# RWKV recurrence on one core: the first group's levels start after its first scores; its transposes and second scores run between them

## The chip, the core and the metric

One of the eight cores of a Trainium2 chip runs the whole kernel. The metric is the device time of one execution in microseconds, the median of several. The engines are TensorE (PE; its weight loads are listed as PEld), VectorE (DVE), ScalarE (ACT), GpSimd (POOL) and SyncE (SP), which issues the DMAs. Each engine works through its own queue in order and waits for the others by semaphores.

## What is computed

A stack of layers over 272 tokens (16 meta tokens and 256) of width 1024: feed-forward blocks, one RWKV-7 time mix, a sparse attention, and a mixer of retention, convolution and block-sparse attention. The change touches only the recurrence of the time mix, for 16 heads of 64:

```python
def step(S, inp):
    r_t, w_t, k_t, v_t, a_t, b_t = inp
    sa = jnp.einsum("bhij,bhj->bhi", S, a_t)
    S = S * w_t[:, :, None, :] + sa[..., None] * b_t[:, :, None, :] + v_t[..., None] * k_t[:, :, None, :]
    y = jnp.einsum("bhij,bhj->bhi", S, r_t)
    return S, y
```

Here `a_t` is minus the normalised key and `b_t` the same key times a gate. To the output `y` a normalisation, a bonus term `sum(r * k * r_k) * v` and a gate are applied, and then the matrix `rk_o`.

## The kernel before, in words

**Tiling.** The recurrence is computed in chunks of tokens, `CHUNKS`: chunk 0 has 16, chunks 1 and 2 have 128 each. Inside a chunk it is a linear system whose matrix is triangular; its inverse is built by doubling, in levels (`rk_levels`, 4 for chunk 0 and 7 for the others). The 16 heads are taken in four groups `g` of four heads (two tiles of 128 rows).

**What a group needs.** `rk_prepare(g)` on DVE scales the operands (five operations of 128x544). `rk_turn(g, c)` on PE transposes six tiles of a chunk into PSUM, and `rk_turned` on ACT copies them out in two copies. `rk_score(g, c, i)` on PE makes the products of the chunk: `i = 0` those from which the inverse is built, `i = 1` those used later, in the chain over chunks. `rk_mask(g, c, i)` on DVE masks each into SBUF. `rk_begin(g, c)` on DVE makes the first approximation of the inverse from the masked `i = 0` product.

**Levels.** In level `n`, `rk_under` (PE) is followed by a copy (ACT, level 0) or a mask (DVE, later), then `rk_merge` (PE) and additions (DVE). The order of chunks is `RK_ORDER = (1, 2, 0)`. `fill` issues dummy matmuls: four before each first product of group 0, and more before level 6. In the first group there are 33 steps on each engine: step 0 to 2 are level 0 (on DVE empty), 3 to 8 level 1 (three products, then three merges), 9 to 14 level 2, 15 to 20 level 3, and four each (chunks 1 and 2) for levels 4, 5 and 6. The first product of level 1 is `rk_under(0,1,1)` (group 0, chunk 1, level 1).

**Order beside the levels.** `beside(host, guest)` puts a second string of work between the steps of the first: the guest yields numbers (ticks), and what comes behind a yield of `k` is issued after step `k`. During the levels of group `g` the guests are the transposes, scores and masks of group `g + 1` and the chain of group `g - 1`. The order is fixed when the program is written; each engine issues it as a single queue.

**Banks.** PSUM has 8 banks. The levels use banks 0 to 4, `rk_banks` gives those of transposes and scores: 6 and 7, and for group 0 chunks 1 and 2 banks 0, 1 and 2, 3. The tiles of `rk_v` before use banks 0 to 2 and the bonus banks 4 to 7 (two halves of DVE's product, `rk_bonus_read`).

**Semaphores.** `rk_masked` counts masks in the order of `MASKS`; `masked(g, c, i)` is the count after that mask. `rk_mask` waits for `rk_products_ready`, before the change by the number `2 * (3 * g + c) + i + 1`.

**Around it.** Before the recurrence stand `rk_r` and `rk_v`, whose weights are split in two parts (`w_high` by ACT, `w_low` by POOL); behind its last group `rk_g2` and `rk_o`, and a feed-forward. The DMA ring of weights is refilled as PE uses slots.

## Time and profile before

| | |
|---|---|
| median of 3 runs | 2140.13 us (2139.15 to 2152.64) |
| profiled execution | 2132.1 us, its span 2130.3 us |
| mean granted TensorE clock | 0.978 of full |
| PE busy | 2013.0 us (94%) |
| DVE / ACT / POOL busy | 1055.2 / 922.0 / 1279.0 us |
| DMA moved | 291.96 MB, 137 GB/s on average |

The profile is that of one execution on the chip. It lists busy times by engine, windows of time with the busy share and the granted clock of TensorE (1.00 is 2.4 GHz, 0.50 is 1.2 GHz), and timelines of instructions. Start times count from the start of the span. Idle time before an instruction is in brackets with what released it. A helper's line (L1916, L1348) stands for many operations; they are told apart by tile and shape. One f32 matmul of the program is two instructions in the trace, so a score of four heads is x8 and an under of a 128-token chunk x16.

### The profile page before, as it was taken

What the parts mean: (1) busy time and instruction counts of PE and PEld (TensorE: products, weight loads), DVE (VectorE), ACT (ScalarE), POOL (GpSimd) and SP (SyncE); (2) the same over time, 40 slices, a digit from 0 to 9 for tenths busy, and PEclk for the clock granted to TensorE, in tenths of its full rate; (3) what the DMA queues carried; (4) which work ended last, traced back from release to release, by engine and by line L of the source; (5) the groups of instructions that cost most, each with busy time, mean ns of one, the idle gap of its engine ahead of it and who ended that gap; (6) DMA issues with size and microseconds to landing.
All of it is one profiled execution on the core that took longest, in us unless ns stands there. A gap on an engine that the chain in (4) does not pass through costs nothing.

```text
span 2130.3 us, 43769 instructions
## 1 busy us (share of the span) xinstructions
PE 2013.0 (94%) x17458; PEld 1896.2 (89%) x17458; DVE 1055.2 (50%) x1623; ACT 922.0 (43%) x1590; POOL 1279.0 (60%) x528
## 2 busy tenths in 40 slices
PE   7999798999999999999978999999999988999997
PEld 7999587778799999999865999989998877898997
DVE  5770766665668716860465577021263244324431
ACT  4333453111343344343436543444446555656552
POOL 6887253000278877786630688967656554677885
PEclk9999899999999999999989999999999999999999
DMA  6444132000244454454320355544354332343552
GB/s 267 170 175 175 73 138 80 3 3 2 80 158 177 166 174 157 177 180 174 125 74 1 139 177 185 192 176 158 125 210 142 139 112 90 135 179 140 191 185 77
DMA packets 40919, 291.96 MB, mean 137 GB/s; under 512 B 4432, under 2 KB 5712, under 8 KB 5712
## 3 DMA queue, kind: packets, MB, share of 16 engines
q1 hardware_dynamic: 40640, 288.92, 38.0%
q8 instruction: 108, 1.77, 0.3%
q10 hardware_dynamic: 144, 1.05, 0.1%
q14 instruction: 27, 0.22, 0.0%
HBM read 288.90 MB, written 1.05 MB: 136 GB/s over the span
## 4 chain that ended last, share of the span: by engine, by line
PE 31%; issue 28%; POOLq 19%; POOL 18%; ACT 1%; DVE 1%; DMA 0%; DVEq 0%; SPq 0%; ACTq 0%
POOLq L1894 18%; POOL w_low L1890 18%; PE ps L587 9%; PE ps L595 9%; PE ps L591 9%; PE ps L1283 1%; PE ps L1271 1%; PE ps L1261 1%; PE ps L699 0%; POOLq L1889 0%; DMA X<-x_in 0%; ACT units L1796 0%; ACT units L1348 0%; POOLq L1906 0%; DVE units L1916 0%
## 5 line engine op out<-in xcount | busy, mean ns | idle before, releaser
L1890 POOL TENSOR_TENSOR w_low<-wring,w_high 128x1024 fp32r<-128x1024 f32 x524 | 1278.8, 2455 | 830.1 <-ACT w_high L1348 800.8
L587 PE MATMUL ps<-in_high,w_high 128*128 128x256 f32 (+1 forms) x2856 | 829.1, 290 | 33.7 <-DVE in_low L1916 12.9
L595 PE MATMUL ps<-in_high,w_low 128*128 128x256 f32 (+1 forms) x2856 | 819.4, 287 | 0.0
L591 PE MATMUL ps<-in_low,w_high 128*128 128x256 f32 (+1 forms) x2856 | 819.3, 287 | 0.0
L1348 ACT ACTIVATE w_high<-wring 128x1024 fp32r<-128x1024 f32 x524 | 542.3, 1055 | 286.4 <-PE ps L587 281.8
L587 PEld LDWEIGHTS ps<-in_high,w_high 128*128 128x128 f32 x2856 | 545.1, 191 | 42.9 <-issue 37.3
L595 PEld LDWEIGHTS ps<-in_high,w_low 128*128 128x128 f32 x2856 | 545.7, 191 | 0.0
L591 PEld LDWEIGHTS ps<-in_low,w_high 128*128 128x128 f32 x2856 | 544.6, 191 | 0.5
L587 PE MATMUL ps<-hid_high,w_high 128*128 128x272 f32 (+1 forms) x880 | 254.9, 290 | 0.0
L595 PE MATMUL ps<-hid_high,w_low 128*128 128x272 f32 (+1 forms) x880 | 250.7, 285 | 0.0
L591 PE MATMUL ps<-hid_low,w_high 128*128 128x272 f32 (+1 forms) x880 | 250.5, 285 | 0.0
L1916 DVE TENSOR_TENSOR hid_low<-hidden,hid_high 128x272 f32 (+1 forms) x88 | 215.7, 2451 | 13.0 <-issue 2.6
L1919 DVE SCALAR_TENSOR_TENSOR X<-ps,X 128x272 f32<-128x272 f32 (+1 forms) x64 | 27.7, 433 | 333.8 <-PE ps L595 333.8
L591 PEld LDWEIGHTS ps<-hid_low,w_high 128*128 128x128 f32 x880 | 165.9, 189 | 0.7
L587 PEld LDWEIGHTS ps<-hid_high,w_high 128*128 128x128 f32 x880 | 165.7, 188 | 0.7
L595 PEld LDWEIGHTS ps<-hid_high,w_low 128*128 128x128 f32 x880 | 165.8, 188 | 0.0
L1490 ACT ACTIVATE silu_out<-ps 128x272 f32<-128x272 f32 (+1 forms) x88 | 34.7, 394 | 301.8 <-DVE ps L1916 301.8
L1954 DVE CAST hid_high<-hidden 128x272 f32 (+1 forms) x88 | 96.7, 1099 | 17.2 <-issue 17.2
L1916 DVE TENSOR_TENSOR ps<-ps,rms 128x272 f32<-128x272 f32 (+1 forms) x176 | 74.0, 436 | 61.6 <-PE ps L595 60.5
L1348 ACT ACTIVATE AL<-ps 128x272 f32<-128x272 f32 (+5 forms) x95 | 39.6, 433 | 142.2 <-PE ps L595 51.9
L1919 DVE SCALAR_TENSOR_TENSOR conv_out<-ps,par,conv_out 128x255 f32<-128x255 f32 x88 | 42.4, 482 | 47.0 <-ACT conv_out L1479 38.3
L1437 ACT ACTIVATE units<-ps 128x256 f32<-128x256 f32 x69 | 26.4, 383 | 85.1 <-PE ps L595 85.0
(331 smaller groups left out, 2580.6 us busy)
## 6 DMA issues: line engine op xcount, KB each, us to landing
wring<-stream SPq DMA_DIRECT2D x271, 1024.0 KB, 4.8
con<-consts SPq DMA_DIRECT2D x1, 2199.0 KB, 16.0
X<-x_in SPq DMA_DIRECT2D x1, 1088.0 KB, 7.6
units<-decay ACTq DMA_DIRECT2D x1, 1024.0 KB, 4.8
out<-AL SPq DMA_DIRECT2D x1, 1024.0 KB, 4.7
par<-params SPq DMA_DIRECT2D x1, 187.0 KB, 4.9
con<-consts SPq DMA_DIRECT2D x1, 130.0 KB, 7.5
```

The costliest lines, as they stand in the source:

```text
L587: mm = pe.matmul(o, wh, high(k), start=(k == 0), stop=False)
L591: mm = pe.matmul(o, wh, low(k), start=False, stop=False)
L595: mm = pe.matmul(o, wl, high(k), start=False, stop=(k == kt - 1))
L1261: mm = pe.matmul(heads(3)[:, q, 0:keys.shape[1]], ns_q[p:p + HD, 2 * g + u, c * P:(c + 1) * P], keys[p:p + HD, :], start=True, stop=True)
L1348: return act.activation(o, i, ACT.Copy, scale=scale)
L1437: act.activation(put(i), ps[:, BANK[tile], 0:size], func(i)).then_inc(S["act_emptied"], 1)
L1490: act.activation(silu_out[:, p % 2, tokens], ps[:, (base + 2 * p) % 4, 0:size], ACT.Silu).then_inc(S["act_emptied"], 1)
L1890: pool.tensor_tensor(w_low[:, (half + h) % SPLIT_RING, :], wring[:, slot, h * HALF * P:(h + 1) * HALF * P], w_high[:, (half + h) % SPLIT_R ...
L1894: pool.drain()
L1916: return dve.tensor_tensor(o, a, b, op)
L1919: return dve.scalar_tensor_tensor(out=o, in0=a, scalar=scalar, in1=b, op0=op0, op1=op1)
L1954: dve.tensor_copy(hid_high[:, tile, tokens], hidden[:, p:p + 1, tokens])
```

## The change

In group 0 the scores `i = 0` come first, in the order of chunks 1, 2, 0, for the first two without waiting for the bonus; DVE begins each chunk behind its mask, and takes the second half of the bonus product between chunk 2 and chunk 0. The transposes of group 0, its scores `i = 1` and their masks move between the levels of group 0, ahead of the same work for group 1, whose ticks move back. Transposes and second scores of all groups now use banks 6 and 7. ACT copies group 0's transposes behind its copies of level 0. DVE's `rk_prepare(1)` stands between the two halves of the bonus.

```diff
--- before.py
+++ after.py
@@ -420,13 +420,13 @@
             bank, at = ((4, 64 * i), (max(i - 1, 0), 0), (2 + max(i - 1, 0), 0))[c]
             return ps[0:C, bank, at:at + 4 * B].rearrange("p (q t) -> p q t", q=4)
 
-        def rk_banks(g, c):
-
-
-            return 6 if g else (6, 0, 2)[c]
-
-
-        MASKS = [(0, c, i) for i in range(2) for c in range(3)]
+        def rk_banks(g, c, i):
+
+
+            return 6 if g or i else (6, 0, 2)[c]
+
+
+        MASKS = [(0, c, 0) for c in RK_ORDER] + [(0, c, 1) for c in range(3)]
         MASKS += [(g, c, i) for g in range(1, 4) for c in range(3) for i in range(2)]
 
         def masked(g, c, i):
@@ -722,16 +722,14 @@
 
                 t0, C = CHUNKS[c]
                 now = slice(t0, t0 + C)
-                before = 3 * g + c
-                if g:
-                    pe.wait_ge(S["rk_masked"], 2 * before)
-                if c == 0:
+                pe.wait_ge(S["rk_masked"], masked(g, c, 0 if g else 1) - 1)
+                if c == 0 and g:
                     pe.wait_ge(S["rk_prepared"], g + 1)
                 settle(C)
                 for i, first in enumerate((32, 8, 16)):
                     for u in range(2):
                         n = 2 * i + u
-                        mm = pe.transpose(ps[0:C, rk_banks(g, c) + n // 4, n % 4 * P:(n % 4 + 1) * P],
+                        mm = pe.transpose(ps[0:C, 6 + n // 4, n % 4 * P:(n % 4 + 1) * P],
                                           A[:, first + 2 * g + u, now], ident)
                 mm.then_inc(S["rk_turned"], 1)
 
@@ -739,15 +737,16 @@
 
                 t0, C = CHUNKS[c]
                 now = slice(t0, t0 + C)
-                before = 3 * g + c
-                if i == 0:
-                    pe.wait_ge(S["rk_tm_copied"], before + 1)
+                if g == i == 0:
+                    pe.wait_ge(S["rk_prepared"], 1)
+                elif g == 0 or i == 0:
+                    pe.wait_ge(S["rk_tm_copied"], 3 * g + c + 1)
                 else:
                     pe.wait_ge(S["rk_masked"], masked(g, c, 0))
                 settle(C)
                 for q, par, u, p in rk_heads:
                     tile = 2 * g + u
-                    o = ps[0:C, rk_banks(g, c) + par, u * 256:(u + 1) * 256].rearrange("p (a t) -> p a t", a=2)[:, :, 0:C]
+                    o = ps[0:C, rk_banks(g, c, i) + par, u * 256:(u + 1) * 256].rearrange("p (a t) -> p a t", a=2)[:, :, 0:C]
                     mm = pe.matmul(o, A[p:p + HD, (32, 8)[i] + tile, now], AL[p:p + HD, 8 + tile:33 + tile:24, now],
                                    start=True, stop=True)
                 mm.then_inc(S["rk_products_ready"], 1)
@@ -757,8 +756,6 @@
                 C = CHUNKS[c][1]
                 if n == 0:
                     pe.wait_ge(S[f"rk_xt{c}_begun"], g + 1)
-                    if g == 0:
-                        pe.wait_ge(S["rk_masked"], masked(g, c, 1))
                     if c == 0 and g >= 2:
                         pe.wait_ge(S["rk_y_rooted"], g - 1)
                 elif n == 1:
@@ -912,6 +909,24 @@
 
 
                 before, after = g - 1, g + 1
+                if g == 0:
+
+
+                    for c, ticks in enumerate(((0, 2), (4, 6), (8, 10))):
+                        yield ticks[0]
+                        rk_turn(0, c)
+                        yield ticks[1]
+                        rk_score(0, c, 1)
+                    for c, ticks in enumerate(((12, 13, 15), (17, 18, 20), (22, 24, 26))):
+                        yield ticks[0]
+                        rk_turn(1, c)
+                        for i in range(2):
+                            yield ticks[1 + i]
+                            if c == 2 and i:
+                                pe.wait_ge(S["rk_x0_added"], RK_COUNT[0])
+                                fill(4, 4)
+                            rk_score(1, c, i)
+                    return
                 if g == 3:
                     pe.wait_ge(S["rk_masked"], len(MASKS))
                 gate = linear_by_two("rk_g1", lambda k: A[:, 40 + k, :]) if g == 3 else iter(())
@@ -1014,12 +1029,10 @@
             beside(split_tiles("rk_v", lambda k: in_high[:, k, :], lambda k: in_low[:, k, :], T,
                                lambda k: pe.wait_ge(S["rk_split"], 2 * DT + k + 1)), rk_bonus())
             pe.wait_ge(*emptied("rk_v", 7))
-            pe.wait_ge(S["rk_bonus_read"], 2)
-            for c in range(3):
-                rk_turn(0, c)
-            for i in range(2):
-                for c in range(3):
-                    rk_score(0, c, i)
+            for c in RK_ORDER:
+                if c == 0:
+                    pe.wait_ge(S["rk_bonus_read"], 2)
+                rk_score(0, c, 0)
             for g in range(4):
                 beside(rk_levels(g), rk_beside(g))
             pe.wait_ge(*emptied("rk_g1", 1))
@@ -1512,9 +1525,9 @@
                 act.wait_ge(S["rk_turned"], 3 * g + c + 1)
                 if g == c == 1:
                     act.wait_ge(S["rk_prepared"], 4)
-                tm, bank = rk_tm[g % 2][c], rk_banks(g, c)
-                copy(tm[0:C, 0:4, :], ps[0:C, bank, :].rearrange("p (a t) -> p a t", a=4))
-                copy(tm[0:C, 4:6, :], ps[0:C, bank + 1, 0:256].rearrange("p (a t) -> p a t", a=2)
+                tm = rk_tm[g % 2][c]
+                copy(tm[0:C, 0:4, :], ps[0:C, 6, :].rearrange("p (a t) -> p a t", a=4))
+                copy(tm[0:C, 4:6, :], ps[0:C, 7, 0:256].rearrange("p (a t) -> p a t", a=2)
                      ).then_inc(S["rk_tm_copied"], 1)
 
             def rk_solved(g, c):
@@ -1606,12 +1619,13 @@
                     act.drain()
                     act.activation(decays, decays, ACT.Exp, scale=-DECAY)
                     act.activation(rk_mid_exp, rk_mid, ACT.Exp, scale=-DECAY).then_inc(S["rk_exps_ready"], 1)
-            for c in range(3):
-                rk_turned(0, c)
             for g in range(4):
                 for c in RK_ORDER:
                     act.wait_ge(S[f"rk_under{c}_ready"], g * RK_LEVELS[c] + 1)
                     copy(rk_x[c][0:CHUNKS[c][1], :, :], rk_level_bank(c, 0)).then_inc(S[f"rk_x{c}_begun"], 1)
+                if g == 0:
+                    for c in range(3):
+                        rk_turned(0, c)
                 for c in range(3):
                     if c and g < 3:
                         rk_turned(g + 1, c - 1)
@@ -2145,11 +2159,7 @@
                 dve.wait_ge(S["rk_exps_ready"], 3)
                 for _ in rk_prepare(0):
                     pass
-                for half in range(2):
-                    v = slice(4 * half, 4 * half + 4)
-                    dve.wait_ge(*emptied("rk_v", 4 * half + 3))
-                    dve.wait_ge(S["rk_bonus_summed"], half + 1)
-                    tt(H[:, v, :], ps[:, 4:8, 0:T], V[:, v, :], ALU.mult).then_inc(S["rk_bonus_read"], 1)
+                rk_bonus_product(0)
                 for _ in rk_prepare(1):
                     pass
                 for c, (t0, C) in enumerate(CHUNKS):
@@ -2161,13 +2171,20 @@
                     dve.tensor_scalar(rk_ends[:, :, :, par], rk_end[:, 0:2, :], head_ones[:, HD * par:HD * par + 1], None,
                                       ALU.mult)
 
+            def rk_bonus_product(half):
+
+                v = slice(4 * half, 4 * half + 4)
+                dve.wait_ge(*emptied("rk_v", 4 * half + 3))
+                dve.wait_ge(S["rk_bonus_summed"], half + 1)
+                tt(H[:, v, :], ps[:, 4:8, 0:T], V[:, v, :], ALU.mult).then_inc(S["rk_bonus_read"], 1)
+
             def rk_mask(g, c, i):
 
                 C = CHUNKS[c][1]
                 mask = tri[0:C, :, 0:C].unsqueeze(1).to_broadcast([C, 4, 2, C])
                 o = (rk_lb, rk_lk)[i][g % 2][c]
-                dve.wait_ge(S["rk_products_ready"], 2 * (3 * g + c) + i + 1)
-                bank = rk_banks(g, c)
+                dve.wait_ge(S["rk_products_ready"], masked(g, c, i))
+                bank = rk_banks(g, c, i)
                 v = ps[0:C, bank:bank + 2, :].rearrange("p b (u a t) -> p (b u) a t", u=2, a=2)[:, :, :, 0:C]
                 tt(o[0:C, :, :, :], v, mask, ALU.mult).then_inc(S["rk_masked"], 1)
 
@@ -2278,7 +2295,16 @@
                 if g == 0:
                     for n in range(2):
                         for i, _ in enumerate(rk_prepare(2 + n)):
-                            yield 3 * n + i + 1
+                            yield 4 * n + i + 1
+                        rk_mask(0, n, 1)
+                    yield 11
+                    rk_mask(0, 2, 1)
+                    for c, ticks in enumerate(((14, 16), (19, 21), (25, 27))):
+                        for i in range(2):
+                            yield ticks[i]
+                            rk_mask(1, c, i)
+                        rk_begin(1, c)
+                    return
                 for c in range(3):
                     if g:
                         yield 7 * c + 1
@@ -2317,13 +2343,11 @@
             residual("ffn_out", 0, factor=0.5)
             rk_norm()
             rk_inputs()
-            for c in range(3):
+            for c in RK_ORDER:
+                if c == 0:
+                    rk_bonus_product(1)
                 rk_mask(0, c, 0)
-            for c in range(3):
-                rk_mask(0, c, 1)
-                if c:
-                    rk_begin(0, c)
-            rk_begin(0, 0)
+                rk_begin(0, c)
             for g in range(4):
                 beside(rk_levels(g), rk_beside(g))
             finish = rk_finish(2)
```

## Rows read from the trace of the kernel before

**Rows 1.** The page: TensorE's line, busy time (share of the span) and instructions.
```profile
PE 2013.0 (94%) x17458; PEld 1896.2 (89%) x17458; DVE 1055.2 (50%) x1623; ACT 922.0 (43%) x1590; POOL 1279.0 (60%) x528
```

**Rows 2.** Windows: us, busy PE, PEld, DVE, ACT, POOL, clock, DMA share, GB/s.
```profile
351.00:368.56 17.56, 13.31 (x131) 10.46 (x131) 15.37 (x30) 3.10 (x8) 0.00 (x0) 0.90 0.00 1
368.56:405.05 36.49, 31.14 (x656) 26.73 (x656) 27.59 (x67) 2.81 (x7) 0.00 (x0) 1.00 0.01 2
```

**Rows 3.** Timeline of TensorE's matmuls: start, duration, what, idle before and releaser.
```profile
352.40 2.13 PE L734 MATMUL ps<-con,AL 128*16 128x128 f32 x18 [1.86 <-DVE AL L1916]
...
362.59 1.93 PE L716 MATMUL ps<-con 128*128 128x128 f32 x8
```

**Rows 4.** Timeline of VectorE, same columns, ahead of the levels.
```profile
341.00 1.28 DVE L1916 TENSOR_TENSOR AL<-ps,AL 128x1088 f32<-128x1088 f32 x1
351.01 1.29 DVE L1916 TENSOR_TENSOR AL<-ps,AL 128x1088 f32<-128x1088 f32 x1 [8.73 <-ACT AL L1348]
352.39 1.36 DVE L1916 TENSOR_TENSOR AL<-AL 128x544 f32<-128x544 f32 x2
...
363.58 1.22 DVE L1916 TENSOR_TENSOR group<-ps,con 128x1024 f32<-128x1024 f32 x1
...
366.09 1.02 DVE L1916 TENSOR_TENSOR group<-group,con 128x256 f32<-128x256 f32 x3
```

**Rows 5.** Timeline of ScalarE: last `rk_v` copy, chunk 0's first copy, a transposed pair.
```profile
350.58 0.40 ACT L1348 ACTIVATE AL<-ps 128x272 f32<-128x272 f32 x1 [2.63 <-PE ps L595]
...
368.67 0.21 ACT L1348 ACTIVATE group<-ps 16x64 f32<-16x64 f32 x1 [0.99 <-PE ps L778]
...
381.72 0.87 ACT L1348 ACTIVATE AL<-ps 128x512 f32<-128x512 f32 x2 [5.06 <-PE ps L734]
```

**Rows 6.** Windows of TensorE alone: us, busy, granted clock, DMA.
```profile
302.30:305.20 2.90, 0.00 (x0) 1.00 0.73 302
...
306.35:313.00 6.65, 6.65 (x26) 0.50 0.41 158
...
357.40:360.85 3.45, 1.30 (x10) 1.00 0.02 5
360.85:364.25 3.40, 3.40 (x16) 0.50 0.00 0
```

**Rows 7.** Timeline of TensorE's weight loads (PEld) in the first group's levels.
```profile
368.56 0.54 PEld L776 LDWEIGHTS ps<-group 64*64 64x64 f32 x16
...
375.70 1.01 PEld L776 LDWEIGHTS ps<-group 64*64 64x64 f32 x32 [0.22 <-DVE group L1916]
...
380.18 0.54 PEld L776 LDWEIGHTS ps<-group 64*64 64x64 f32 x16
...
388.19 0.54 PEld L776 LDWEIGHTS ps<-group 64*64 64x64 f32 x16
389.70 0.64 PEld L734 LDWEIGHTS ps<-con,AL 128*128 128x128 f32 x6 [0.96 <-DVE AL L1916]
390.50 0.54 PEld L776 LDWEIGHTS ps<-group 64*64 64x64 f32 x16 [0.17 <-issue]
...
392.05 0.73 PEld L751 LDWEIGHTS ps<-AL 64*128 64x128 f32 x8
...
394.04 0.55 PEld L776 LDWEIGHTS ps<-group 64*64 64x64 f32 x16
...
399.78 0.97 PEld L716 LDWEIGHTS ps<-con 128*128 128x128 f32 x8
...
405.05 0.43 PEld L778 LDWEIGHTS ps<-con,in_parts 64*64 64x64 f32 x11
```

**Rows 8.** Timeline of VectorE in the levels: small mask, pair of additions, level mask.
```profile
380.48 0.27 DVE L1916 TENSOR_TENSOR in_parts<-ps,con 16x128 f32<-16x128 f32 x1
...
386.71 0.74 DVE L1916 TENSOR_TENSOR group<-ps,group 128x256 f32<-128x256 f32 x2
...
389.57 0.40 DVE L1916 TENSOR_TENSOR in_parts<-ps,con 128x256 f32<-128x256 f32 x1
```

## The prediction

> **What bounds the kernel now.** I read the page first: TensorE (PE) is busy 94% of the span [rows 1], and the weight stream, its split on POOL and the matmuls pace nearly everything. The recurrence is the exception, so the windows by stage came next. Between the last matmul of `rk_v` (about 350.5 us) and the first level of the inverse, PE is busy 13.3 of 17.6 us and VectorE (DVE) 15.4 of 17.6; inside the first group's levels PE is busy 31.1 and DVE 27.6 of 36.5 [rows 2]. POOL stands still and the DMA moves almost nothing in both: no weights are split here, so every microsecond that the levels end sooner or later moves all that comes after by as much. The timelines of the engines then show the order. The reader is to see three marks: PE's first transpose at 352.40 [rows 3], the first level-1 product `rk_under(0,1,1)` at 368.56 and the first product of group 1 at 405.05 [rows 7]. The change acts between the first and the last of them.
>
> Up to 352.3 DVE sets the pace: it waits for the last `rk_v` copy of ScalarE (ACT), multiplies the bonus (1.29 us) and prepares group 1 [rows 4, 5]. Then masks and beginnings alternate with PE's scores; PE's first level waits for them and starts behind its fill, which ends at about 364.5 [rows 3].
>
> **Ahead of level 0.** PE no longer waits for the bonus. `rk_prepare(1)` and the ends (from 352.39, five operations of 0.68 us and seven small ones, some 4.3 us together) go to the wait before the last copy of `rk_v`, where DVE was idle for 8.73 us (342.28 to 351.01) [rows 4]; without that cover they would cost their 4.3 us. The two scores of chunks 1 and 2 need only banks 0 to 3, which the last copy (ended 350.98) frees [rows 5]. At 1.06 us each (392.05 to 394.04 is a score and a merge) [rows 7], slightly more for the first, they run from 351.0 to 353.2. DVE: chunk 1's mask starts at 352.2. A mask with its beginning takes from 363.58 to about 366.45 (the first of the three merged operations at 366.09 belongs to it), so 2.9 us [rows 4]. Two of them: 358.0. Then the second bonus product, 1.29: 359.3. What is moved behind it is the point: `rk_score(0,0,0)` waits for that product, and PE's queue holds it before `rk_under(0,1,0)`, whose input has been ready since 355.1. So level 0 does not begin at 355.1 but at 359.6 plus its fill. PE idles from 353.2 to 359.3.
>
> **PE's clock.** An idle stretch of 2.9 us (302.3 to 305.2) was followed 1.2 us later by the lower level, 1.2 GHz, for 6.65 us [rows 6]. The thin stretch 357.4 to 360.85 (PE busy 1.3 of 3.45 us) was followed by 3.4 us at half clock [rows 6]. An idle stretch of 6.1 us will do so too, so PE resumes at 1.2 GHz. How long it stays there is not known: in the before it came back 3.5 us after dense work had begun again (360.7 to 364.25), in the other place 7.8 us (305.2 to 313.0) [rows 6]. I take 4 us, near the one in the same place, and keep 7.8 and "no fall" for the range. At half clock a fill of four took 1.93 us [rows 3], at full clock 0.97 of issue (399.78) [rows 7].
>
> PE from 359.3: score of chunk 0 (0.5), fill (1.9), `rk_under(0,1,0)` (1.1 slow, against 0.54) to 362.8. Next, at tick 0, six transposes of chunk 0 (0.8 fast, 389.70 to 390.50 [rows 7], here 1.1) to 363.9; fill 0.97, chunk 2's product 0.55, fill 0.97, chunk 0's product 0.3: 366.7. And then a new wait: `rk_score(0,0,1)` at tick 2 needs the transposes copied, and ACT takes them only after its copy of chunk 0's first product (0.21), 0.87 for the pair [rows 5]. Its end is about 367.9, the score takes 0.3, and level 1 begins at 368.2. **Term 1: 368.2 against 368.56, -0.4 us.** DVE meanwhile is idle: `rk_prepare(2)` (3.4 us for five operations, as rk_prepare(1) from 352.39) ends at 364.2.
>
> At this place a rule of the skill bears. The row first: at 389.70 PE started chunk 1's transposes after 0.96 us of idleness, though chunk 2's product behind them (390.50) had its input since 387.45 [rows 7, 8]. The Trainium skill ("TensorE: Matmul & The Clock Gate", section "Step-by-step: what each phase is for") says that only weight loads are pulled ahead and matmuls stay in program order. The trace agrees. Were it otherwise, level 0 would start 4.5 us earlier and the sum would be that much lower; by the rule it is as I have it.
>
> **Beside the levels.** The levels now carry three sets of transposes, the second scores (0.3, 1.06, 1.06 us) and three more masks (0.27 [rows 8], 1.22 and 1.22 [rows 4]); of this 4.6 us is PE's and 2.7 DVE's. In return DVE has `rk_prepare(2)` behind it. Whether this is hidden is decided by who waits for whom, so I laid out both queues with the durations of the rows: an under of a 128-chunk 0.54, of chunk 0 0.25, a merge 1.0 (390.50 to 392.05 is an under and a merge) [rows 7], a pair of additions 0.74, a level mask 0.4 [rows 8], a pair of copies 0.87 [rows 5]. All banks of the side work are 6 and 7, so it forms one string: transposes, copy, score, mask, next transposes. Counted from level 1's start, t:
>
> - Level 1, to `rk_under(0,1,2)`: before 7.14 us [rows 7], there DVE-bound. After: PE waits for mask (0,0,1) until t+1.4, transposes to 2.25, chunk 0's product 2.5, merge 3.5, score (0,1,1) 4.55, merges of chunks 2 and 0 to 5.9, then transposes (0,2) wait for mask (0,1,1). That mask sits on DVE behind `rk_prepare(3)` and chunk 2's addition (6.85) and ends at 8.0. Transposes to 8.85. **+1.7.**
> - Level 2, before 4.48 (375.70 to 380.18). After: products and score (0,2,1) to 11.25, merge 12.25, then transposes (1,0) wait for mask (0,2,1), over at 12.8; to 13.6; merges and score (1,0,0) to 15.25. 6.4. **+1.9.**
> - Level 3, before 8.01 (380.18 to 388.19). After: score (1,0,1) waits to 16.0, transposes (1,1) to 17.65, and score (1,1,1) for mask (1,1,0), which now stands behind chunk 2's addition: over at 23.5. Level 4 starts at 24.6; 9.35. **+1.35.**
> - Level 4, before 5.85. After: transposes (1,2) wait for mask (1,1,1), 26.9, then merge, merge, score: 31.05; 6.45. **+0.6.**
> - Level 5 to the fill of level 6, before 5.74 (394.04 to 399.78). After: mask (1,2,1) stands behind chunk 1's additions and ends at 37.8. 6.8. **+1.05.**
> - Level 6 to group 1, before 5.27 (399.78 to 405.05). The additions of chunk 1 are already done this time; chunk 2's end at 40.7; group 1 starts at 42.1. 4.25. **-1.0.**
>
> Sum of the levels: 1.7 + 1.9 + 1.35 + 0.6 + 1.05 - 1.0 = +5.6 us; with term 1, **+5.2 us**. Group 1 starts at about 410.3 instead of 405.05. Later groups keep their order, banks and counts: 0. By the profiled execution (2132.1 us, span 2130.3) that gives 2137.3; the median of the runs is 2140.13, 8 us above that execution, so I add the difference to the median: **2145.3 us**.
>
> **The rivals.**
> - *Low clock for 7.8 us* (to 367.1): fills, product and transposes at half rate until then make t 370.0 instead of 368.2. +7.0: 2147.1. For it: 306.35 to 313.0 [rows 6]; against it, the same place of the before.
> - *No fall of the clock*: t 366.4, +3.4: 2143.5. Against it: none of the stretches as thin as this one kept the full clock [rows 6].
> - *The side work is hidden* (the other side: faster). PE is idle 5.35 and DVE 8.9 us of the 36.5 [rows 2], against 4.6 and 2.7 us of added work. If my waits on masks overlap better than laid out, the levels keep 36.5 us, and with t between 366.4 and 368.2 the gain is 0.4 to 2.2 us: 2138 to 2140. It decides if the levels grow by less than 0.4 us; against it stand the three waits (mask (0,1,1), (0,2,1), (1,1,0)) of 1.7 to 2.1, 0.6 and 1.7 us in PE's queue.
> - *The start is what counts*: level 0 really begins when chunk 1 is ready, at 355.1, which takes 4.5 us off everything: 2140.8, no change. Program order speaks against it.
> - *A loss of over 21 us* would need later stages to lose their pace, e.g. low clock around each small wait; the order, banks and counts of groups 1 to 3 are untouched, and a shift alone does not do that.
>
> **How the numbers follow.** Forecast 0.55, with a range of its own from 2142 to 2149; longer low clock 0.15; no fall 0.05; side work hidden 0.14; start counts 0.07; something larger 0.04. The range takes in the hidden case and the long clock; the two close runs of the before differ by 1 us and the third lies 12 above, so I leave some room above: 2137 to 2152. A measurement tells about 1% (21 us) from no change; all cases but the last stay inside: faster 0.02, same 0.95, slower 0.03.
>
> **What would show it.** Right: scores at 351.0, then PE idle for about 6 us up to the chunk 0 score near 359.3; half clock behind it; level 1 near 368; 41 to 43 us of levels with PE waiting for DVE's masks before transposes; group 1 near 410. Wrong: levels of 37 us (hidden), a first product at 355 (order), or groups 1 to 3 of other length than before (then I missed an effect behind the levels).

## The result: 0.6% slower, and the profile after

| | before | changed |
|---|---|---|
| median | 2142.31 us (20 runs) | 2157.09 us (20 runs) |
| lowest to highest | 2136.97 to 2158.57 | 2146.96 to 2167.43 |
| ratio | | 1.0061, 95% interval 1.0042 to 1.0079 |
| profiled execution, its span | 2132.1, 2130.3 us | 2156.98, 2155.2 us |
| mean granted clock in it | 0.978 | 0.969 |

Ratios and means leave out the slow executions, those more than 1.5% above the fastest of their kernel; in all that follows these are three of the twelve of e1_fill, the profiled one among them. The ratio is worth 13 us (9 to 17), against 5.2 forecast. The change is within 1%, but the median lies 5 us above the range, and the loss is about two and a half times the forecast.

The two profiled executions differ by 24.9 us, and not all of it belongs to the change. I cut the span at events that both traces have. The first is ScalarE's last copy of `rk_v`, which in the changed kernel reads:

```profile
358.01 0.40 ACT L1361 ACTIVATE AL<-ps 128x272 f32<-128x272 f32 x1 [2.63 <-PE ps L595]
```

Its answer in [rows 5] is at 350.58. So 7.4 of the 24.9 us are there before any edited instruction runs; they come and go with the clock in the stages before (a table follows below). From there the changed kernel can be read against [rows 7]. The timeline of TensorE's weight loads, changed kernel:

```profile
358.46 1.60 PEld L750 LDWEIGHTS ps<-AL 64*128 64x128 f32 x16 [0.71 <-ACT AL L1361]
366.76 0.26 PEld L750 LDWEIGHTS ps<-AL 64*16 64x16 f32 x8 [6.70 <-issue]
367.11 1.78 PEld L716 LDWEIGHTS ps<-con 128*128 128x128 f32 x8
369.11 0.93 PEld L775 LDWEIGHTS ps<-con,group 64*64 64x64 f32 x16 [0.22 <-issue]
...
375.90 0.20 PEld L750 LDWEIGHTS ps<-AL 64*16 64x16 f32 x8 [1.21 <-issue]
376.15 1.01 PEld L773 LDWEIGHTS ps<-group 64*64 64x64 f32 x32
...
384.00 0.64 PEld L732 LDWEIGHTS ps<-con,AL 128*128 128x128 f32 x6 [1.68 <-DVE group L1930]
384.81 1.01 PEld L773 LDWEIGHTS ps<-group 64*64 64x64 f32 x32 [0.17 <-issue]
...
391.40 0.54 PEld L773 LDWEIGHTS ps<-group 64*64 64x64 f32 x16
...
399.90 0.73 PEld L750 LDWEIGHTS ps<-AL 64*128 64x128 f32 x8 [1.80 <-DVE AL L1930]
400.96 1.01 PEld L773 LDWEIGHTS ps<-group 64*64 64x64 f32 x32 [0.33 <-issue]
...
407.59 1.01 PEld L773 LDWEIGHTS ps<-group 64*64 64x64 f32 x32 [0.33 <-issue]
...
414.69 0.97 PEld L716 LDWEIGHTS ps<-con 128*128 128x128 f32 x8 [1.76 <-DVE AL L1930]
415.78 0.54 PEld L769 LDWEIGHTS ps<-group 64*64 64x64 f32 x8
416.38 1.70 PEld L716 LDWEIGHTS ps<-con 128*128 128x128 f32 x8
...
420.41 0.43 PEld L775 LDWEIGHTS ps<-con,in_parts 64*64 64x64 f32 x11
```

Line 750 is a score, 716 a fill, 775 a product of level 0, 773 one of a later level, 732 the transposes. The reader sees the two scores at 358.5, the 6.7 us of idleness behind them, chunk 0's score at 366.76 and, behind a fill at half clock (1.78 instead of 0.97), level 0 at 369.11: 10.7 us behind the end of the last copy (358.41), where the kernel before needed 13.5 (350.98 to 364.45). By level 1 (376.15) this lead is gone. The waits of 1.68 us (transposes for mask (0,1,1)), 1.80 (score (1,1,1) for mask (1,1,0)) and 1.76 (level 6 for mask (1,2,1)) are the three longest in the levels; one of 1.33 (transposes at 403.30 for mask (1,1,1)) follows them. Windows of the same kernel, TensorE alone (us, busy, granted clock, DMA):

```profile
412.70:414.70 2.00, 0.38 (x12) 1.00 0.00 0
414.70:416.40 1.70, 1.70 (x17) 1.00 0.00 0
416.40:419.80 3.40, 3.40 (x25) 0.51 0.00 0
...
560.00:563.40 3.40, 2.74 (x23) 0.98 0.12 19
563.40:573.60 10.20, 10.20 (x71) 0.50 0.25 98
573.60:580.00 6.40, 6.40 (x77) 1.00 0.01 3
```

Behind the wait at 412.7 the clock fell once more, and it fell again for 10.2 us in the last part of the recurrence, where the trace of before has 1.00 throughout.

Where the 24.9 us went, in the two traces: 7.4 ahead of the change; 0.2 up to level 1 (376.15 - 358.01 = 18.1 against 368.56 - 350.58 = 18.0); 7.8 in the levels (420.41 - 376.15 = 44.3 against 36.5); 1.1 in groups 1 to 3; 3.4 in the last chain ahead of `rk_o`; 5.0 behind that, which I have not followed up. The 1.1 and the 3.4 lie in the one stretch at half clock. VectorE's rows of the kernel before, and then the same two of the changed kernel:

```profile
535.16 0.42 DVE L1916 TENSOR_TENSOR group<-ps,group 128x256 f32<-128x256 f32 x1 [1.77 <-PE ps L798]
...
557.99 0.42 DVE L2224 COPY in_parts<-ps 128x256 f32<-128x256 f32 x1 [1.43 <-PE ps L837]
```

```profile
550.53 0.42 DVE L1930 TENSOR_TENSOR group<-ps,group 128x256 f32<-128x256 f32 x1 [1.77 <-PE ps L795]
...
577.92 0.42 DVE L2241 COPY in_parts<-ps 128x256 f32<-128x256 f32 x1 [1.42 <-PE ps L834]
```

At the opening of group 1 (406.20 and 421.56) the changed kernel is 15.36 us behind, at the first of these rows 15.37, at the second 19.93. So groups 1 to 3 ran exactly as before until the clock fell at 563.4.

### The profile page after: what moved, and what is told of

Same layout as the page of the kernel before. It is cut to its first block, busy times and chain, and to the rows that moved or that the text cites. A ratio compares the mean times of both kernels' runs of the same rounds, so it can differ in the third digit from the quotient of the medians.

```text
span 2155.2 us, 43767 instructions
## 1 busy us (share of the span) xinstructions
PE 2030.9 (94%) x17458; PEld 1911.0 (89%) x17458; DVE 1056.9 (49%) x1623; ACT 922.1 (43%) x1590; POOL 1275.8 (59%) x528
## 4 chain that ended last, share of the span: by engine, by line
PE 31%; issue 29%; POOLq 19%; POOL 18%; ACT 1%; DVE 1%; DMA 0%; DVEq 0%; SPq 0%; ACTq 0%
POOLq L1908 18%; POOL w_low L1904 18%; PE ps L587 9%; PE ps L595 9%; PE ps L591 9%; PE ps L1296 1%; PE ps L1284 1%; PE ps L1274 1%; PE ps L699 0%; POOLq L1903 0%; DMA X<-x_in 0%; ACT units L1810 0%; ACT units L1361 0%; POOLq L1920 0%; DVE units L1930 0%
```

## Two measures for the experiments

**Marks.** For each trace three distances. *Start*: from the start of ScalarE's last `rk_v` copy to VectorE's first level-1 mask (before: 350.58 to 370.55). *Levels*: from there to VectorE's first copy of the chain, which opens group 1 (before: 406.20). *Groups 1 to 3*: from there to POOL's first split for `rk_o` (before: 551.81). These marks come out equal to 0.05 us between traces of kernels that do the same thing at the same clock. They are these rows of VectorE and POOL, first of the kernel before:

```profile
370.55 0.42 DVE L1916 TENSOR_TENSOR in_parts<-ps,con 128x256 f32<-128x256 f32 x1
...
406.20 0.41 DVE L2224 COPY in_parts<-ps 16x256 f32<-16x256 f32 x1 [0.42 <-PE ps L837]
```

```profile
551.81 2.35 POOL L1890 TENSOR_TENSOR w_low<-wring,w_high 128x1024 fp32r<-128x1024 f32 x1 [211.32 <-ACT w_high L1348]
```

and of the changed kernel:

```profile
376.88 0.42 DVE L1930 TENSOR_TENSOR in_parts<-ps,con 128x256 f32<-128x256 f32 x1 [5.27 <-PE ps L773]
...
421.56 0.41 DVE L2241 COPY in_parts<-ps 16x256 f32<-16x256 f32 x1 [0.42 <-PE ps L834]
```

```profile
568.30 2.35 POOL L1904 TENSOR_TENSOR w_low<-wring,w_high 128x1024 fp32r<-128x1024 f32 x1 [220.38 <-ACT w_high L1361]
```

**Time at low clock.** Each timed run lists its span s and mean granted clock c, and the clock has two levels, 1.2 and 2.4 GHz. So 2 x (1 - c) x s is the time spent at 1.2 GHz. Over the runs of one kernel, the time rises by 0.29 to 0.46 us for each microsecond of it (least squares). I give the mean of it, and the time that the line gives at 110 us of low clock, so that kernels can be compared at the same share of low clock. The three values for the kernel before belong to the comparisons of e1 to e4, of e5 to e8 and of e9 to e12. The marks are from one trace each.

| kernel | runs | ratio (interval) | start | levels | groups 1 to 3 | low clock, mean | time at 110 us low |
|---|---|---|---|---|---|---|---|
| before | 29 to 35 per comparison | 1 | 20.0 | 35.7 | 145.6 | 118, 107, 110 | 2139.2, 2138.7, 2139.1 |
| changed | 20 | 1.0061 (1.0042 to 1.0079) | 18.9 | 44.7 | 146.7 | 141 | 2145.8 |
| changed, once more | 1 | | 18.4 | 48.8 | 157.7 | 151 | |
| e1_fill | 9 of 12 | 1.0060 (1.0031 to 1.0089) | 16.5 | 48.6 | 157.7 | 136 | 2145.9 |
| e2_bonus_first | 10 | 1.0068 (1.0041 to 1.0096) | 13.6 | 47.8 | 155.1 | 143 | 2144.2 |
| e3_before_plus8 | 12 | 1.0011 (0.9989 to 1.0033) | 24.1 | 35.7 | 145.6 | 107 | 2144.5 |
| e4_prepare_early | 12 | 0.9993 (0.9968 to 1.0017) | 20.0 | 35.7 | 145.6 | 112 | 2140.5 |
| e5_masks_early | 12 | 1.0018 (1.0001 to 1.0036) | 18.3 | 41.7 | 145.6 | 111 | 2140.3 |
| e6_both | 11 | 1.0023 (1.0001 to 1.0046) | 14.8 | 40.1 | 150.6 | 122 | 2141.0 |
| e7_fill_waits | 12 | 1.0029 (1.0011 to 1.0046) | 16.5 | 43.8 | 154.0 | 109 | 2144.6 |
| e9_wait_counts | 12 | 1.0001 (0.9982 to 1.0019) | 17.8 | 37.6 | 145.6 | 108 | 2139.2 |
| e10_mixed_start | 12 | 0.9979 (0.9956 to 1.0002) | 15.1 | 35.7 | 149.6 | 111 | 2136.7 |
| e11_last_mask | 12 | 1.0052 (1.0031 to 1.0073) | 19.0 | 42.1 | 149.5 | 128 | 2142.2 |
| e12_before_late_mask | 12 | 1.0045 (1.0015 to 1.0075) | 20.0 | 36.9 | 150.3 | 125 | 2141.2 |

The changed kernel is 6.6 to 7.1 us slower than before at equal low clock. How much more low clock it has must be estimated: the 20 runs of the kernel before in its own comparison are on record without their clocks, and the later sets of the kernel before differ by 11 us among themselves. On the lines of those sets, the mean of the 20 runs, 2144.1 us, belongs to about 125 us of low clock. By that estimate the changed kernel has some 16 us more, worth 6 us at 0.37 us each (the slope of its own 20 runs). The two parts add to the 13 us: about half is order and waits, about half the clock.

## The experiments

My theory at the outset: the order of the queues costs what the marks show, and the low clock is a second cost that follows from TensorE's thin stretches. Rivals: the clock is all of it; the added work as such is the cost; a shift of the recurrence costs more than itself in the stages behind.

**e3_before_plus8: does a delay cost more than itself?**

```diff
                         if g == n == 0:
-                            fill(4, 4)
+                            fill(4, 37 if c == 1 else 4)
```

> The kernel before with 33 more dummy matmuls (8.0 us at full clock) ahead of the first product of level 0, all else as it was. Theory (a delay in the recurrence is handed on one to one): levels of 36.5 us, all stages behind as long as before, +8 us, ratio 1.0037. Rival (a delay there costs more than itself, because later stages meet the clock or the weight stream otherwise): +12 to +14 us, ratio 1.006, with the excess visible behind the recurrence.

The start grew by 4.1 us, not 8. The low clock of the before ahead of level 0 was gone, and the first level-1 product came 5.3 us later. In the kernel before VectorE, still at `rk_prepare(2)`, took up the mask behind that product only 2.0 us after the product's start (368.56 to 370.55); here it had idled for 3.99 us and took it up after 0.7. Levels and groups 1 to 3 were the same to 0.03 us. The time at equal low clock rose by 5.3 us and the low clock fell from 118 to 107, so the ratio came to 1.0011, less than I had expected. The rival falls: a dense delay is handed on about one to one and disturbs nothing behind it.

**e1_fill: TensorE kept busy in its idle 6 us.**

```diff
                 if c == 0:
+                    pe.wait_ge(S["rk_masked"], 1)
+                    fill(0, 24)
                     pe.wait_ge(S["rk_bonus_read"], 2)
```

> The changed kernel with 24 dummy matmuls (some 5.8 us at full clock) between the second and the third score, behind the first mask, so that TensorE does not idle while VectorE masks and multiplies the bonus. Theory (order and waits, the low clock is a side effect): the low clock from 365 to 374 goes, the stretch from the last rk_v copy to the first level-1 product falls from 18.1 to about 16.3 us, the levels stay at 43 to 44 us; total 2 us under the changed kernel, so a ratio to before of about 1.005. Rival (the clock is the whole loss): the ratio to before falls to 1.000.

The start fell by 2.4 us (18.9 to 16.5), a little more than expected. But the ratio stayed at 1.0060, which neither theory nor rival had: in this trace the clock fell at the end of the levels and stayed low for 23.9 us. Low clock was 136 us a run beside 118 of before in the same comparison, an excess like that of the changed kernel. That a fall mended at one place comes at the next thin one fits this; one trace does not show it.

**e2_bonus_first: what holds level 0.**

```diff
+            rk_bonus_product(1)
             for c in RK_ORDER:
-                if c == 0:
-                    rk_bonus_product(1)
                 rk_mask(0, c, 0)
```

> The changed kernel with VectorE's second bonus product ahead of the first mask instead of behind the second chunk's beginning. Theory (TensorE's queue holds the third score, and behind it level 0, until the bonus is read): the third score moves up from 8.3 us behind the last rk_v copy to about 2.2, level 0 starts when chunk 1's beginning is done, some 5 us behind the copy instead of 11, the first level-1 product comes at 13 to 14 us instead of 18.1, the levels stay at 43 to 44 us; total 4 to 5 us under the changed kernel, ratio to before about 1.003 to 1.004. Rival (VectorE's own work sets level 0, the place of the bonus does not matter): 18 us as before.

The start is 13.6 us, 5.3 less than in the changed kernel: chunk 0's score in TensorE's queue was indeed what held level 0. In time it brought nothing (1.0068). The levels of this trace are 3.1 us longer, groups 1 to 3 are 8.3 us longer, with one low stretch of 27 us, 53 us behind the copy. Low clock was 143 us a run beside 118. Theory right on the queue, wrong on the total (1.003 to 1.004 was expected).

**e8_after_again: the changed kernel, a second trace.**

> The changed kernel once more, unaltered, for a second trace. Both theories expect the same waits to within 0.3 us: some 18 us from the last rk_v copy to the first level-1 product and about 41 to 44 us of levels. If the low-clock stretches lie at the same distance from the start of the recurrence as in the first trace (beside level 0, at the end of the levels, ahead of rk_o), they belong to the order of work; if they lie elsewhere, their place is chance and only their number can be compared.

The waits are the same, the start 18.4. The clock is not: the same wait ahead of level 6 is followed by 23.9 us at 1.2 GHz instead of 3.4, through the end of the levels and into group 1. Windows of TensorE:

```profile
398.00:405.00 7.00, 6.90 (x124) 1.00 0.01 2
405.00:407.00 2.00, 0.38 (x4) 1.00 0.00 0
407.00:408.30 1.30, 1.30 (x16) 1.00 0.00 0
408.30:432.20 23.90, 23.78 (x305) 0.50 0.01 1
```

and the cause of the wait, VectorE in the same trace:

```profile
404.17 1.19 DVE L1930 TENSOR_TENSOR group<-ps,group 64x256 f32<-64x256 f32 x3 [1.98 <-PE ps L795]
405.39 1.23 DVE L1930 TENSOR_TENSOR AL<-ps,con 128x1024 f32<-128x1024 f32 x1
```

The additions of level 5 come first, then the mask for which TensorE waits. In the kernel before this mask stands ahead of the additions:

```profile
398.39 1.22 DVE L1916 TENSOR_TENSOR AL<-ps,con 128x1024 f32<-128x1024 f32 x1
...
401.23 2.40 DVE L1916 TENSOR_TENSOR group<-ps,group 64x256 f32<-64x256 f32 x6
```

The low-clock stretches of the two traces lie at the same places (beside level 0, at the end of the levels, ahead of `rk_o`) and differ in length: 6.8, 3.4 and 10.2 us against 6.8, 23.9 and 17.1, with two more of 3.4 in the levels of the second.

**e5_masks_early: the masks ahead of the additions.**

```diff
-                    for c, ticks in enumerate(((14, 16), (19, 21), (25, 27))):
+                    for c, ticks in enumerate(((14, 16), (18, 21), (24, 26))):
```

> The changed kernel with three of group 1's masks on VectorE one step earlier (ticks 18 instead of 19, 24 instead of 25, 26 instead of 27), so that each stands ahead of the additions of level 3 and 5 that it stood behind. Theory (the levels are long because TensorE's queue waits for these masks, and the clock falls in these waits): the levels shrink from 44.3 to 39 to 41 us, no low clock at their end, time at low clock back from 141 to about 120 us a run, ratio to before 1.001 to 1.003. Rival (the added work itself, 4.6 us on TensorE, is the cost): levels 43 us or more, ratio 1.006 as the changed kernel.

Three numbers on VectorE took two thirds of the loss: ratio 1.0018, low clock 111 us a run beside 107 of before in the same comparison, levels 41.7, and groups 1 to 3 at 145.6. What is left (start and levels together 60.0 against 55.6, 4.3 us in the trace) I put down to the added string beside the levels; no run takes it apart. The theory holds: the late masks make most of the loss, partly directly (the levels by 3 us in the traces), partly by the clock (3 us more low clock than before, where the changed kernel has some 16).

**e11_last_mask: one of the three alone.**

```diff
-                    for c, ticks in enumerate(((14, 16), (19, 21), (25, 27))):
+                    for c, ticks in enumerate(((14, 16), (19, 21), (25, 26))):
```

> The changed kernel with a single mask one step earlier: group 1, chunk 2, second score, tick 26 instead of 27, so that the wait of TensorE ahead of level 6 (1.8 us in the trace) goes. Theory (this wait is where the clock falls and then stays low, up to 24 us in some runs): levels 42 to 43 us, time at low clock in the recurrence 7 to 14 us instead of 20 to 55, a ratio of 1.003 to 1.004. Rival (all the thin places count alike): levels 43 to 44, ratio 1.005 to 1.006.

Levels 42.1 as expected, low clock 128 us beside 110, ratio 1.0052. Its trace has no fall at the end of the levels, but one of 17.1 us ahead of `rk_o`. So the wait ahead of level 6 is not the only source of low clock. Whether it is one stays undecided: the interval (1.0031 to 1.0073) does not tell this kernel from the changed one.

**e12_before_late_mask: the same delay put into the kernel before.**

```diff
-                        yield 24 + 2 * i
+                        yield 24 + 2 * i + (g == 0)
```

> The kernel before with only this one mask later, and its neighbour (group 1, chunk 2: ticks 25 and 27 instead of 24 and 26), as the changed kernel has them. Theory: the levels grow by 1.5 to 3 us, and the low clock behind them appears, with 5 to 20 us more at 1.2 GHz a run; ratio 1.001 to 1.004. Rival (the low clock comes from other waits of the changed kernel or from chance): levels at most 1.5 us longer, time at low clock as in the kernel before, ratio 1.0005.

Two masks (both of group 1, chunk 2) come one tick later. The levels grew by 1.2 us, less than the theory's 1.5 to 3, the whole by 0.45% (some 10 us), with 125 us of low clock beside 110. About 2 us are there at equal low clock, 15 us of low clock are worth 5 to 6. In the trace the fall is again not in the levels but ahead of `rk_o` (17.1 us). That late masks in the levels bring low clock is supported in the mean (125 +- 6 against 110 +- 3, one standard error each), that it does so in the very wait is not: the place varies.

**e7_fill_waits: dummy matmuls in all these waits** (24 ahead of the third score as in e1_fill, and 2 to 6 ahead of each wait beside the levels).

```diff
+                        if c:
+                            fill(5, 3 * c)
                         rk_turn(0, c)
...
+                        fill(5, (2, 2, 4)[c])
                         rk_turn(1, c)
...
+                            if c == i == 1:
+                                fill(5, 5)
...
+                        if n == LEVELS - 1 and g == 0 and c == 1:
+                            fill(5, 6)
```

> The changed kernel with dummy matmuls in all of TensorE's waits that the trace shows: 24 in the idle 6 us ahead of the third score, and 2 to 6 ahead of each wait for a mask beside the levels of group 0. They take only time in which TensorE waited. Theory (half of the loss is the clock, which falls behind thin stretches): no low clock from 358 to 425 us, time at low clock back to about 120 us a run, ratio 1.002 to 1.003, the remaining 5 to 6 us being waits. Rival (the clock's extra 23 us at 1.2 GHz come from elsewhere, by chance): ratio 1.006 unchanged.

The low clock went back to 109 us a run, as in the before of its comparison (107), and the ratio to 1.0029; at equal low clock it stays 5.9 us above the before. This agrees with the estimate above: waits and order about 6 us, the clock behind them the other half. Its own trace still has a fall of 17 us at the end of the levels, so the fills go with less low clock in the mean and do not exclude a fall.

**e6_both: bonus first and masks early,** the edits of e2_bonus_first and e5_masks_early together.

```diff
+            rk_bonus_product(1)
             for c in RK_ORDER:
-                if c == 0:
-                    rk_bonus_product(1)
...
-                    for c, ticks in enumerate(((14, 16), (19, 21), (25, 27))):
+                    for c, ticks in enumerate(((14, 16), (18, 21), (24, 26))):
```

> Both mends: the bonus product ahead of the first mask and the three masks one step earlier. Theory: first level-1 product 4 to 5 us nearer to the last rk_v copy than in the changed kernel (as the bonus-first kernel showed), levels of 39 to 41 us; together the first product of group 1 at the place of the kernel before or up to 2 us earlier, and low-clock time like the kernel before: ratio 0.998 to 1.001. Rival (the clock falls anyway, as in the bonus-first kernel with its 24 us at 1.2 GHz): ratio 1.004 or more with time at low clock over 135 us.

Start 14.8 and levels 40.1 make 54.9, 0.7 us less than before. The ratio was 1.0023, with 122 us of low clock; at equal low clock 2.3 us above before. The ratio lies between what theory and rival had said, and so does the low clock: less than the rival's 135 us, more than the 107 of before.

**e4_prepare_early and e9_wait_counts: the one part of the change that looks free.** The first moves `rk_prepare(1)` into VectorE's idle time and leaves TensorE's order as it was:

```diff
                 for _ in rk_prepare(0):
                     pass
-                for half in range(2):
...
+                rk_bonus_product(0)
                 for _ in rk_prepare(1):
                     pass
...
             rk_inputs()
+            rk_bonus_product(1)
             for c in range(3):
                 rk_mask(0, c, 0)
```

The second has the same edit and adds

```diff
-                dve.wait_ge(S["rk_products_ready"], 2 * (3 * g + c) + i + 1)
+                dve.wait_ge(S["rk_products_ready"], masked(g, c, i))
```

> The kernel before with one part of the change alone: VectorE prepares group 1 between the two halves of the bonus, in its 8.7 us of idle time; TensorE's order is untouched. Theory (VectorE paced the stretch ahead of level 0): the masks start about 1.5 us earlier, when TensorE's transposes, copies and scores are there, and the first level-1 product comes at 15 to 16.5 us behind the last rk_v copy instead of 18.0; levels 36.5 us; ratio 0.999. Rival (TensorE's transposes and scores paced it as well): 17.5 to 18 us, no gain.

> The kernel before with the early preparation of group 1, and in addition each mask waits for its own score instead of for the number 2 * (3 * g + c) + i + 1 (which makes chunk 1's first mask wait for three scores and chunk 2's for five). Theory (the gain of the early preparation was eaten by these counts): chunk 1's mask starts 0.9 us earlier and chunk 2's follows it without the 1.24 us of idleness; level 0 and the first level-1 mask come 1.5 to 2.5 us earlier than in the early-preparation kernel, levels 35.7 us, ratio 0.998 to 0.9995. Rival (TensorE's fills at the low clock set level 0): less than 0.5 us.

The early preparation gained nothing: start 20.0 as before. VectorE now waited for scores (2.5 and 1.9 us ahead of its first two masks) where it had worked; the 1.2 us ahead of the third were there before. With the right counts the start fell by 2.2 us, as expected; and the levels grew by 2.0 (37.6), so nothing came of that either (1.0001). In its trace TensorE ran at half clock from 367.6 to 374.4 us, at the beginning of the levels, where the before had 1.00; the before's low stretch, ahead of level 0, was gone. Both are misses in time.

**e10_mixed_start: a third order.** First scores of chunks 1 and 2 early, bonus ahead of the masks, all second scores ahead of the levels (those of chunks 1 and 2 in banks 0 to 3), only two sets of transposes beside the levels. On TensorE:

```diff
             pe.wait_ge(*emptied("rk_v", 7))
+            rk_score(0, 1, 0)
+            rk_score(0, 2, 0)
             pe.wait_ge(S["rk_bonus_read"], 2)
-            for c in range(3):
-                rk_turn(0, c)
-            for i in range(2):
-                for c in range(3):
-                    rk_score(0, c, i)
+            rk_turn(0, 0)
+            rk_score(0, 0, 0)
+            for c in RK_ORDER:
+                rk_score(0, c, 1)
```

> A third order: the first scores of chunks 1 and 2 right behind rk_v as in the changed kernel, but the bonus product ahead of the masks, all second scores ahead of the levels in banks 0 to 3 as in the kernel before, and only the transposes of chunks 1 and 2 beside the levels (ticks 0 and 5). Theory (the start gains when VectorE is fed early, the levels lose by second scores and masks in one pair of banks): first level-1 mask 5 us nearer to the last rk_v copy than in the kernel before (15 instead of 20), levels of 36 to 38 us, no long stretch of low clock, ratio 0.997 to 0.999. Rival (what starts earlier is given back in the levels whatever stands beside them): levels of 40 us or more and ratio 1.000 or above.

The start is 15.1 us and the levels 35.7, as in the kernel before: 4.8 us less, and this time nothing given back in the levels. TensorE kept the full clock through both; the only low stretch of this recurrence, 17.1 us, lies ahead of `rk_o`. VectorE works in one unbroken string from the bonus on.

```profile
356.02 1.29 DVE L1930 TENSOR_TENSOR AL<-ps,AL 128x1088 f32<-128x1088 f32 x1 [4.28 <-ACT AL L1360]
357.23 1.22 DVE L1930 TENSOR_TENSOR group<-ps,con 128x1024 f32<-128x1024 f32 x1
...
363.73 2.53 DVE L1930 TENSOR_TENSOR group<-ps,con 128x1024 f32<-128x1024 f32 x3
366.35 1.36 DVE L1930 TENSOR_TENSOR AL<-AL 128x544 f32<-128x544 f32 x2
```

The ratio is 0.9979 (0.9956 to 1.0002), the best of all, and its interval reaches 1: clearly faster than the changed kernel, not told apart from the kernel before. It keeps the early first scores of the change and leaves out the late bonus and the second scores and masks of group 0 beside the levels; several things differ at once, so which of them gave what is not shown.

## Why the prediction was wrong, step by step

- **What bounds it** and **the start**: right. PE idle from 353.2 to 359.3 was forecast, 6.1 us; it was 6.7. The queue (third score ahead of level 0) was confirmed by e2_bonus_first. Term 1 was -0.4 and measured +0.2, with low clock for 6.8 us instead of 4.
- **Beside the levels**, counted from level 1's start, forecast and measured: 8.85 and 8.66; 6.4 and 6.59; 9.35 and 9.56; 6.45 and 6.63; 6.8 and 7.10; 4.25 and 5.72. The first five are within 0.3 us each and 0.7 together. Laying out two in-order queues with the durations of the rows is good enough for this, and the named waits (1.7, 1.7 us and the mask behind the additions) are in the trace.
- **Level 6** (-1.0) is a term that was mis-sized: it measured +0.45. I had seen that TensorE would wait for mask (1,2,1), and did not ask what 1.8 us of idleness does to the clock there. The second fill took 1.70 instead of 0.97 us.
- **"Later groups keep their order, banks and counts: 0"** is the step that failed. They kept all three, and still took 1.1 and 3.4 us more up to `rk_o` in the first trace, all of it in the stretch at 1.2 GHz from 563.4 to 573.6, and over 10 in the second, with 1.2 GHz up to 432.2 and again ahead of `rk_o`. In the mean of the runs the extra low clock is worth about 6 of the 13 us; the order and the waits, at 6.6 to 7.1 us, were near the 5.2 forecast. I had priced the clock in one place, the idle 6 us that I had found, and nowhere else.
- **The rival "a loss ... low clock around each small wait"** named the mechanism, and I put 0.04 on it, arguing that "a shift alone does not do that". That is true of a shift (e3_before_plus8), but the change is not a shift: it makes waits.
- **The start is what counts**: no. Level 0 came behind chunk 0's score (366.76, then 369.11), as program order has it.
- **The side work is hidden**: no. **No fall of the clock**: no. **Low clock for 7.8 us**: near at the start (6.8), but small beside what came behind.
- **The range** took its width from the local bounds. The two sources it left out are the low clock of the levels and of the later groups.

## What stays open

The means go with about 16 us more low clock in the changed kernel and hardly any once the masks are early or the waits filled (3 and 1 us), but the timed runs give only a total, so where in the kernel this low clock lies is known from single traces alone. Why a fall lasts 3.4 us in one trace and 23.9 in another behind the same wait, and why it often comes ahead of `rk_o`, where the instructions are those of the kernel before, I cannot say either. The fall there was absent from the traces of before, e3_before_plus8, e4_prepare_early, e5_masks_early and e9_wait_counts, and present (10.2 or 17.1 us) in the nine others. That goes roughly with whether the clock was disturbed, but e7_fill_waits and e10_mixed_start have it too, with 109 and 111 us of low clock in the mean like the before; so one trace is one draw. Open too are the 5.0 us behind `rk_o` in the first trace, and whether e10_mixed_start beats the kernel before.

## What to carry to other kernels

When side work goes between the steps of a latency chain, lay out both queues and put the producer of each awaited operand ahead of the chain's own step, not behind it: two masks one step later cost 0.45% (0.15 to 0.75), some 10 us, where the levels in the trace grew by 1.2. A wait of 1.8 us on TensorE in a part that is already thin was followed by 3.4 us of low clock in one trace and 23.9 in another; price such waits with the low clock that may follow, here and in the stages behind. A start that comes earlier is worth only what the queues behind it do not give back. In comparing two traces, first subtract what differs ahead of the change.

## What the hardware showed that I had not expected

The granted clock fell to 1.2 GHz for 23.9 us while TensorE was busy for 23.78 of them (408.30 to 432.20), mostly with the small matmuls (64 or 16 wide) of the recurrence; after the idle stretch at 302.3 us of the before it came back after 6.65 us [rows 6]. It is not a matter of small matmuls alone: e4_prepare_early, with nothing changed there, ran at half clock for 34.0 us from 1576.4 on, TensorE busy for 32.9 of them, most of it in dense 128*128 products. The traces of e1_fill and e6_both have a stretch as long near the same place, the other eleven none over 6.8 us there. So here a busy share near 1 did not say that the clock would return soon. The unchanged part ahead of the change differed by 11 us between traces: the last `rk_v` copy came at 347.0 to 347.6 (five traces), 350.6 to 351.3 (five), 355.5 to 358.0 us (four), with 20, 27 and 34 to 38 us of low clock ahead of it. Such steps, which have nothing to do with the change, are part of the spread of this kernel's runs.
